# Attention of one encoder layer: softmax denominators on 128 partitions, a second PV result buffer, and a new order of taps, copies and the last quarter

## The chip, the cores and the metric

The kernel runs on one core of one Trainium2 chip. The metric is the device time of one execution in microseconds (us), as the median of three runs. A difference of about 0.3% (5.8 us) is what can be told from no change. The engines are named as the profile names them: PE (matmul), PEld (its weight loads), DVE (vector), ACT (scalar activations), POOL (GpSimd), SP (which only issues transfers here).

## The reference, cut to what matters

One encoder layer on 1024 tokens of width 1024. Between two feed-forward blocks stands a mixer whose input projection feeds two groups: a depthwise convolution of 31 taps on 512 channels, and an attention of eight heads. The change touches the attention and what is interleaved with it.

```python
def one_block(qblk):
    s = jnp.einsum('bqhd,bkhd->bhqk', qblk, k, preferred_element_type=jnp.float32) * scale
    p = jax.nn.softmax(s, axis=-1).astype(v.dtype)
    return jnp.einsum('bhqk,bkhd->bqhd', p, v)
...
a = u[..., :C_CONV] * jax.nn.sigmoid(u[..., C_CONV:])
a = lax.conv_general_dilated(a, conv_w[i], ...) + conv_b[i]     # 31 taps, depthwise
a = jax.nn.silu(_layernorm(a, g_conv_ln[i], b_conv_ln[i]))
...
mix = jnp.concatenate([a, att], axis=-1) @ w_out[i]
```

## The kernel before, in words

All engines run programs written out by hand, each in its own order; semaphores tie them together. The attention is cut into four **turns** (`i`, two heads each) of four **quarters** (`m`, one head and one half of the 512 queries each; `m` even is the first half of a head, `m` odd the second), and each quarter into four **parts** (`p`). `run_units` writes turn 0 and turn 3 out and loops over turns 1 and 2, calling each engine's own `unit`.

What PE does in a part: in even quarters it first transposes a quarter of the next head's q and k (L1710, four matmuls, into PSUM bank 7); then the scores of the next quarter once in low precision for the row maxima (`pe_max`, L1594, two matmuls); the scores proper (`pe_scores`, L1635, six matmuls); and two of the eight key tiles of PV (`pe_pv`, L1657, four matmuls into bank 6) for the quarter before. In part 3 the PV is split in two, and between the halves PE transposes the four columns of maxima into a row (`pe_max_row`, L1616).

What serves it: DVE reduces the maxima (`dve_max`, L1602) and takes the rounding rests of the transposed head (`dve_head_unit`, L1728) after ACT has copied it (`act_head_unit`, L1721). ACT copies the row of maxima (`act_max`, L1623), then takes the exponentials (`act_exp`, L1644). The values matrix carries 64 columns of ones, so that rows 0 to 63 of bank 6 are the PV result and rows 64 to 127 are 64 equal copies of the denominators, for 512 queries.

The end of a quarter's PV, in `m`'s part 3 and the next quarter: `act_pv_copy` (L1666) copies bank 6 to SBUF (`grow`) in one 128x512 instruction; `dve_pv_recip` (L1673) inverts rows 64 to 127 in three pieces of 192, 160 and 160 columns, written to rows 0 to 63; `dve_pv_scale` (L1681) multiplies 64x512 into `att`. There is one buffer, so the copy waits for the scale of the quarter before (`pv_out`), and PE's next PV waits for the copy (`pv_copied`) and for the exponentials (`s_exp`).

Interleaved is the convolution. In turns 0 to 2 ACT multiplies (`act_prod`, L1806, 10 products of 128x1024 in each head; part 3 has one, part 0 of an even quarter two) into a ring of two, and POOL adds each in two halves of 128x512 (L1815, L1816). `act_prod` waits until POOL has added the product before last. DVE does four further taps in each odd quarter (`dve_tap`, L1826, 128x1024). POOL also prepares the next head's q and k (L1760, L1762, L1766) in odd quarters. In turn 3 there are no taps and products; POOL sums and scales for the layer norm of the convolution (L1850) and scales `w_out` rows as they arrive (L1910), ACT and DVE cut them in high and low parts (L1920, L1924), DVE scales the convolution by the norm (`dve_ln_scale`, L1895), and ACT applies the swish (L1901). After the last quarter PE does the PV of the last one and goes on to the output projection (L2759), whose left operand DVE cuts from `cv` and `att` (`cut_mix`, L2565 and L2568).

## Time and profile before

| quantity | us |
|---|---|
| median of three runs | 1916.84 |
| lowest, highest run | 1915.08, 1920.34 |
| the profiled execution, its own time | 1917.73 |
| span of its profile | 1915.9 |
| mean granted TensorE clock | 0.986 of full |

A timeline row reads: start, duration of the group, engine and line, operation, what is written and read, how many, and in brackets how long the engine sat idle before it and who ended that. Consecutive instructions of one line are merged; an instruction's record starts about 0.1 us before its predecessor's record ends. PE records overlap further, so that the pitch (start to start) tells more than the duration.

### The profile page before, as it was taken

Reading aid. Unit: us, or ns where it says so; the run is one execution under the profiler, and the core shown is the slowest. Engines: PE = TensorE matmul, PEld = TensorE weight load, DVE = VectorE, ACT = ScalarE, POOL = GpSimd, SP = SyncE. Lnnn points to the kernel's source line nnn. Section 1 sums busy time; section 2 is a strip of 40 time slices with the busy share of each in tenths; the row PEclk is TensorE's granted clock in tenths of the full one; section 3 lists DMA queues with packets and bytes.
Section 4 is the critical chain, followed back from the end, with each engine's and each line's share of the span. In section 5 each row is a group of like instructions: output and inputs, shape, how many; then the busy total and the mean of one; then the engine's idle time right before and its main releaser. Section 6 shows DMA issues by size and latency. Waiting matters only on the chain.

```text
span 1915.9 us, 22675 instructions
## 1 busy us (share of the span) xinstructions
PE 1839.0 (96%) x8039; PEld 1469.6 (77%) x8039; DVE 1386.3 (72%) x1774; ACT 797.3 (42%) x1252; POOL 803.2 (42%) x605
## 2 busy tenths in 40 slices
PE   4999999999999999997999999999999999999997
PEld 3788888888888878985655666877888888888886
DVE  6678888886777785776888886358656555577778
ACT  4532232223344554237676653154332333334443
POOL 1076655665200010019999952014566556520000
PEclk9999999999999999997999999999999999999999
DMA  9046666545753442000000024112233323476333
GB/s 352 16 139 198 210 219 203 193 155 199 254 205 94 122 173 65 8 1 0 1 1 0 0 66 154 66 56 93 100 111 109 110 83 110 171 253 225 98 106 126
DMA packets 132795, 232.11 MB, mean 121 GB/s; under 512 B 8780, under 2 KB 66227, under 8 KB 132434
## 3 DMA queue, kind: packets, MB, share of 16 engines
q1 hardware_dynamic: 132500, 230.73, 35.7%
q8 instruction: 62, 1.02, 0.2%
q14 instruction: 43, 0.35, 0.1%
q10 hardware_dynamic: 190, 0.01, 0.0%
HBM read 177.75 MB, written 52.95 MB: 120 GB/s over the span
## 4 chain that ended last, share of the span: by engine, by line
PE 36%; POOL 7%; issue 6%; DVE 5%; ACT 1%; DMA 1%; POOLq 0%; ACTq 0%; DVEq 0%
PE ps L502 19%; PE ps L854 9%; PE ps L2759 5%; POOL cv L1816 3%; PE ps L1657 1%; POOL cv L1815 1%; PE ps L376 1%; POOL slot L1766 1%; PE ps L1635 1%; DVE T L935 1%; POOL rqk L1751 0%; DVE ring L479 0%; POOL slot L1762 0%; DVE H L2605 0%; POOL slot L1760 0%
## 5 line engine op out<-in xcount | busy, mean ns | idle before, releaser
L502 PE MATMUL ps<-T,ring 128*128 128x512 f32 x1920 | 441.8, 389 | 0.0
L502 PEld LDWEIGHTS ps<-T,ring 128*128 128x128 f32 x1920 | 360.4, 188 | 74.9 <-DVE ring L479 0.2
L502 PE MATMUL ps<-B,ring 128*128 128x512 f32 x1440 | 339.7, 392 | 4.6 <-DVE SG L561 3.7
L502 PEld LDWEIGHTS ps<-B,ring 128*128 128x128 f32 x1440 | 270.6, 189 | 64.4 <-issue 8.5
L954 POOL TENSOR_SCALAR stat<-stat 128x1 f32<-128x1 f32 x32 | 10.1, 315 | 548.2 <-ACT XS L879 258.8
L568 POOL TENSOR_TENSOR HID<-HID,SG 128x512 f32<-128x512 f32 x80 | 122.1, 1526 | 263.0 <-DVE HID L553 152.2
L854 PE MATMUL ps<-PW 128*128 128x512 f32 x924 | 217.3, 389 | 0.0
L854 PE MATMUL ps<-PT 128*128 128x512 f32 x900 | 212.0, 390 | 0.0
L854 PEld LDWEIGHTS ps<-PW 128*128 128x128 f32 x924 | 173.3, 188 | 36.0
L479 DVE TENSOR_TENSOR ring<-sums,ring 128x512 fp32r<-128x512 f32 x160 | 162.3, 1023 | 52.9 <-ACT ring L473 52.9
L854 PEld LDWEIGHTS ps<-PT 128*128 128x128 f32 x900 | 168.5, 188 | 34.7
L473 ACT ACTIVATE ring<-sums 128x512 fp32r<-128x512 f32 x160 | 97.1, 627 | 162.4 <-PE ps L502 144.5
L522 ACT ACTIVATE SG<-SG 128x512 f32<-128x512 f32 x80 | 50.6, 633 | 242.5 <-DVE SG L553 96.4
L1657 PE MATMUL ps<-E,vs 128*128 128x512 f32 x256 | 125.6, 606 | 5.6 <-ACT grow L1666 5.6
L479 DVE TENSOR_TENSOR ring<-rawu,ring 128x512 fp32r<-128x512 f32 x60 | 66.9, 1125 | 51.6 <-ACT ring L473 51.6
L1635 PE MATMUL ps<-qkT 97*128 97x512 f32 x384 | 102.3, 403 | 0.0
L701 ACT ACTIVATE PW<-adat 128x512 fp32r<-128x512 f32 x77 | 48.6, 631 | 123.4 <-PE ps L854 87.4
L1602 DVE TENSOR_REDUCE negmax<-ps 128x1 f32<-128x1024 f32 x64 | 76.8, 1203 | 30.5 <-PE ps L1594 30.4
L701 ACT ACTIVATE PT<-adat 128x512 fp32r<-128x512 f32 x75 | 47.4, 631 | 107.7 <-PE ps L854 92.1
L708 DVE TENSOR_TENSOR PT<-adat,PT 128x512 fp32r<-128x512 f32 x84 | 58.7, 708 | 43.2 <-ACT PT L701 43.2
L1816 POOL TENSOR_TENSOR cv<-cv,prod 128x512 f32<-128x512 f32 x60 | 89.6, 1494 | 0.0
L1635 PEld LDWEIGHTS ps<-qkT 97*128 97x128 f32 x384 | 73.8, 193 | 19.1 <-ACT qkT L1623 1.2
(337 smaller groups left out, 3307.6 us busy)
## 6 DMA issues: line engine op xcount, KB each, us to landing
adat<-ffn_hidden SPq DMA_DIRECT2D x154, 256.0 KB, 2.7
ada_raw<-in_w_ada SPq DMA_DIRECT2D x56, 512.0 KB, 4.0
rawg<-in_ffn_wg SPq DMA_DIRECT2D x22, 1024.0 KB, 5.5
rawu<-in_ffn_wu SPq DMA_DIRECT2D x22, 1024.0 KB, 5.2
ffn_hidden<-HID SPq DMA_DIRECT2D x84, 256.0 KB, 2.7
ffn_hidden<-base SPq DMA_DIRECT2D x66, 256.0 KB, 2.9
H<-in_x SPq DMA_DIRECT2D x16, 512.0 KB, 6.2
h_saved_rows<-H SPq DMA_DIRECT2D x16, 512.0 KB, 2.6
```

The source lines that it names most:

```text
L473: e.activation(ring[:, n % RING, HI], src, ACT.Copy).then_inc(f.w_hi.sem, 1)
L479: e.tensor_tensor(ring[:, n % RING, LO], src, ring[:, n % RING, HI].bitcast(F32), ALU.subtract).then_inc(f.w_lo.sem, 1)
L502: mm = e.matmul(ps[:, product_bank(M, k)], ring[:, place % RING, wx, kc], RIGHT[k][:, xx, kc], start=(kc == 0 and i == 0), stop=(kc == HC ...
L568: e.tensor_tensor(HID[:, q], HID[:, q], SG[:, q], ALU.mult).then_inc(f.w_mul.sem, 1)
L701: e.activation(pair(f, n)[:, 0, HI], left_raw(n), ACT.Copy).then_inc(f.cut_hi.sem, 1)
L708: e.tensor_tensor(pair(f, n)[:, side, LO], raw, pair(f, n)[:, side, HI].bitcast(F32), ALU.subtract)\
L854: mm = e.matmul(bank_of(j, t), pair(f, n)[:, 0, ax, t * P:(t + 1) * P], pair(f, n)[:, 1, wx], start=(g == 0 and i == 0), stop=(g == GROUPS ...
L1602: e.tensor_reduce(negmax[:, m % 2, p:p + 1], ps[:, b:b + NH].rearrange("p b k -> p (b k)"), AX_X, ALU.max, negate=True).then_inc(s_max, 1)
L1635: mm = e.matmul(ps[:, 2 + 2 * (p % 2) + b], qkT[0:AUG, hp, 1, x, kt * P:(kt + 1) * P], qkT[0:AUG, hp, 0, y, h * HALF:(h + 1) * HALF], star ...
L1657: mm = e.matmul(ps[:, 6], vs[:, hp, kt], EX[(m - 1) % 2][:, kt], start=(kt == 0), stop=(kt == NT - 1))
L1816: e.tensor_tensor(cv[:, c, second_half], cv[:, c, second_half], prod[:, n % 2, second_half], ALU.add)\
L2759: mm = e.matmul(ps[:, 4 + m % MB], mixT[:, t % 2, xx, c], wo[:, c, wx, h * HALF:(h + 1) * HALF], start=(c == 0 and k == 0), stop=(c == KC ...
```

## The change

Six things, all in the attention:

- the copy of the PV result becomes four instructions of 64x256: result and denominators of 256 queries go to rows 0 to 63 and those of the other 256 queries to rows 64 to 127, of two separate arrays in `grow`;
- each array has two buffers (`m % 2`), so the copy waits for the scale of two quarters before;
- the reciprocal is in place on 128 partitions, two pieces of 128 columns instead of three of 192, 160 and 160 on 64;
- the scale is two instructions of 64x256, done in part 2 instead of part 3;
- ACT does the copy ahead of the part's exponential instead of after it (not in the last quarter of the last turn); the DVE tap of an odd quarter's part 3 moves to the same place as those of the other parts;
- in the last turn the reciprocals and the scale of quarter 3 are all in part 0, around the two small layer norm steps, and the four layer norm scalings all in part 2.

```diff
         def act_pv_copy(e, i, m):

             e.wait_ge(pv_mm, i * 4 + m)
-            if not (isinstance(i, int) and i == 0 and m == 1):
-                e.wait_ge(pv_out, i * 4 + (m - 1))
-            e.activation(grow[:, 0:HALF], ps[:, 6], ACT.Copy).then_inc(pv_copied, 1)
+            if not (isinstance(i, int) and i == 0 and m <= 2):
+                e.wait_ge(pv_out, i * 4 + (m - 2))
+            for c in range(2):
+                of_ps = slice(c * QUERIES, (c + 1) * QUERIES)
+                for to, rows in ((pv_res, slice(0, VH)), (pv_sum, slice(VH, 2 * VH))):
+                    copied = e.activation(to[c * VH:(c + 1) * VH, m % 2], ps[rows, 6, of_ps], ACT.Copy)
+            copied.then_inc(pv_copied, 1)
...
-            a, b = ((0, 192), (192, 352), (352, HALF))[third]
-            e.reciprocal(grow[0:VH, HALF + a:HALF + b], grow[VH:2 * VH, a:b]).then_inc(pv_rec, 1)
+            x = pv_sum[:, m % 2, part * P:(part + 1) * P]
+            e.reciprocal(x, x).then_inc(pv_rec, 1)
...
-            e.tensor_tensor(dst, grow[0:VH, 0:HALF], grow[0:VH, HALF:D], ALU.mult).then_inc(pv_out, 1)
+            for c in range(2):
+                at_q = h * HALF + c * QUERIES
+                dst = att[hp * VH:(hp + 1) * VH, bass.ds(chunk, 1), at_q:at_q + QUERIES].rearrange("p a q -> p (a q)")
+                half = slice(c * VH, (c + 1) * VH)
+                scaled_rows = e.tensor_tensor(dst, pv_res[half, m % 2], pv_sum[half, m % 2], ALU.mult)
+            scaled_rows.then_inc(pv_out, 1)
...
+                    if p == 3 and not (first and m == 0) and not (last and m == 3):
+                        act_pv_copy(e, i, m)
                     act_exp(e, i, m, p)
-                    if p == 3 and not (first and m == 0):
+                    if last and (m, p) == (3, 3):
                         act_pv_copy(e, i, m)
...
-                    elif not last and p < 3:
+                    elif not last:
                         dve_tap(e, i * DTT + (DT + m // NH * 2 + p // 2), (p % 2,))
...
+                        elif not at_end and p < 2:
                             dve_pv_recip(e, *at(i, m - 1), p)
...
+                        elif not at_end and p == 2:
+                            dve_pv_scale(e, *at(i, m - 1))
```

How the rows move on DVE in an odd quarter, turn 0, quarter 3 (`negmax` the maxima of the next quarter, `cv<-ac,cw,cv` a tap, `grow` the denominators, `att` the scaled result). Before:

```order
L1602 TENSOR_REDUCE negmax<-ps 128x1
L1826 SCALAR_TENSOR_TENSOR cv<-ac,cw,cv 128x1024
L1673 RECIPROCAL grow<-grow 64x192
L1602 TENSOR_REDUCE negmax<-ps 128x1
L1826 SCALAR_TENSOR_TENSOR cv<-ac,cw,cv 128x1024
L1673 RECIPROCAL grow<-grow 64x160
L1602 TENSOR_REDUCE negmax<-ps 128x1
L1826 SCALAR_TENSOR_TENSOR cv<-ac,cw,cv 128x1024
L1673 RECIPROCAL grow<-grow 64x160
L1602 TENSOR_REDUCE negmax<-ps 128x1
L1681 TENSOR_TENSOR att<-grow 64x512
L1826 SCALAR_TENSOR_TENSOR cv<-ac,cw,cv 128x1024
```

The same quarter after:

```order
L1602 TENSOR_REDUCE negmax<-ps 128x1
L1838 SCALAR_TENSOR_TENSOR cv<-ac,cw,cv 128x1024
L1681 RECIPROCAL grow<-grow 128x128
L1602 TENSOR_REDUCE negmax<-ps 128x1
L1838 SCALAR_TENSOR_TENSOR cv<-ac,cw,cv 128x1024
L1681 RECIPROCAL grow<-grow 128x128
L1602 TENSOR_REDUCE negmax<-ps 128x1
L1838 SCALAR_TENSOR_TENSOR cv<-ac,cw,cv 128x1024
L1692 TENSOR_TENSOR att<-grow 64x256 x2
L1602 TENSOR_REDUCE negmax<-ps 128x1
L1838 SCALAR_TENSOR_TENSOR cv<-ac,cw,cv 128x1024
```

One reciprocal less stands ahead of the last maxima of the quarter, and the scale now stands behind the third tap instead of ahead of the fourth.

On ACT at the seam of two quarters, turn 0, part 3 of quarter 2 into quarter 3 (`qkT` the row of maxima, then `E` the exponentials, `prod` a product for POOL). Before:

```order
L1623 ACTIVATE qkT<-ps 1x512
L1644 ACTIVATE E<-ps 128x1024
L1666 ACTIVATE grow<-ps 128x512
L1806 ACTIVATE prod<-ac,cw 128x1024
L1644 ACTIVATE E<-ps 128x1024
```

After:

```order
L1623 ACTIVATE qkT<-ps 1x512
L1673 ACTIVATE grow<-ps 64x256 x4
L1644 ACTIVATE E<-ps 128x1024
L1818 ACTIVATE prod<-ac,cw 128x1024
L1644 ACTIVATE E<-ps 128x1024
```

The copy, four instructions now, stands between the row of maxima and the part's exponential; the product stays behind both.

On DVE in quarter 3 of the last turn and what follows it (`stat` the layer norm's variance, `wo` the low part of a `w_out` row block, `cv<-cv,ps` the layer norm scaling). Before:

```order
L1881 TENSOR_REDUCE stat<-ps 128x8
L1883 TENSOR_SCALAR stat<-stat 128x8
L1673 RECIPROCAL grow<-grow 64x192
L1924 TENSOR_TENSOR wo<-wor,wo 128x1024
L1673 RECIPROCAL grow<-grow 64x160
L1924 TENSOR_TENSOR wo<-wor,wo 128x1024
L1673 RECIPROCAL grow<-grow 64x160
L1895 TENSOR_TENSOR cv<-cv,ps 128x1024 x2
L1924 TENSOR_TENSOR wo<-wor,wo 128x1024
L1681 TENSOR_TENSOR att<-grow 64x512
L1895 TENSOR_TENSOR cv<-cv,ps 128x1024 x2
```

After:

```order
L1681 RECIPROCAL grow<-grow 128x128
L1893 TENSOR_REDUCE stat<-ps 128x8
L1895 TENSOR_SCALAR stat<-stat 128x8
L1681 RECIPROCAL grow<-grow 128x128
L1692 TENSOR_TENSOR att<-grow 64x256 x2
L1936 TENSOR_TENSOR wo<-wor,wo 128x1024 x2
L1907 TENSOR_TENSOR cv<-cv,ps 128x1024 x4
L1936 TENSOR_TENSOR wo<-wor,wo 128x1024
```

The scale of quarter 3 moves from the last but one place to ahead of the first of three `wo` cuts.

## Rows read from the trace of the kernel before

**Rows 1.** The page, part 1: busy time, share of the span, instructions.

```profile
PE 1839.0 (96%) x8039; PEld 1469.6 (77%) x8039; DVE 1386.3 (72%) x1774; ACT 797.3 (42%) x1252; POOL 803.2 (42%) x605
```

**Rows 2.** Windows (us, busy of each engine, PEclk, DMA): one head of turn 2.

```profile
1056.00:1089.00 33.00, 31.36 (x118) 19.59 (x117) 28.73 (x25) 23.19 (x28) 31.79 (x23) 1.00 0.00 0
```

**Rows 3.** Timeline of PE, turn 2, second head.

```profile
1064.43 0.64 PE L1710 MATMUL ps<-ident,slot 128*96 128x128 f32 x4 [0.93 <-DVE qkT L1728]
...
1071.84 0.65 PE L1616 MATMUL ps<-ident,negmax 128*128 128x128 f32 x4
1072.33 1.02 PE L1657 MATMUL ps<-E,vs 128*128 128x512 f32 x2
...
1075.04 1.88 PE L1657 MATMUL ps<-E,vs 128*128 128x512 f32 x4
...
1087.41 0.65 PE L1616 MATMUL ps<-ident,negmax 128*128 128x128 f32 x4 [0.65 <-DVE negmax L1602]
```

**Rows 4.** Timeline of ACT, same stretch.

```profile
1061.87 1.15 ACT L1806 ACTIVATE prod<-ac,cw 128x1024 f32 x1 [1.34 <-POOL cv L1816]
...
1073.14 1.03 ACT L1644 ACTIVATE E<-ps 128x1024 f32<-128x1024 f32 x1
1074.06 0.59 ACT L1666 ACTIVATE grow<-ps 128x512 f32<-128x512 f32 x1
1074.54 1.16 ACT L1806 ACTIVATE prod<-ac,cw 128x1024 f32 x1
```

**Rows 5.** Timeline of POOL, same stretch.

```profile
1067.84 1.28 POOL L1816 TENSOR_TENSOR cv<-cv,prod 128x512 f32<-128x512 f32 x1
...
1075.77 1.65 POOL L1815 TENSOR_TENSOR cv<-cv,prod 128x512 f32<-128x512 f32 x1 [1.21 <-ACT prod L1806]
...
1087.36 3.00 POOL L1816 TENSOR_TENSOR cv<-cv,prod 128x512 f32<-128x512 f32 x1
```

**Rows 6.** Timeline of DVE, same stretch.

```profile
1071.04 0.75 DVE L1728 SCALAR_TENSOR_TENSOR qkT<-ps,gains,qkT 96x512 fp32r<-96x512 f32 x1 [0.23 <-ACT qkT L1721]
...
1075.00 1.28 DVE L1826 SCALAR_TENSOR_TENSOR cv<-ac,cw,cv 128x1024 f32<-128x1024 f32 x1
...
1087.32 0.68 DVE L1681 TENSOR_TENSOR att<-grow 64x512 f32 x1
```

**Rows 7.** Groups with shapes apart: count, busy us, mean ns, idle before.

```profile
L1666 ACT ACTIVATE grow<-ps 128x512 f32<-128x512 f32 x16 | 9.5, 592 | 6.8 <-DVE att L1681 5.1 <-PE ps L1657 1.7
...
L2212 ACT ACTIVATE tmp<-ps 128x256 f32<-128x256 f32 x8 | 3.1, 391 | 0.0
...
L1673 DVE RECIPROCAL grow<-grow 64x160 f32<-64x160 f32 x32 | 36.3, 1140 | 0.8
...
L2463 DVE TENSOR_TENSOR rt<-kr 128x256 f32<-128x256 f32 x1 | 0.4, 419 | 0.0
```

**Rows 8.** Timeline of all engines, last turn, quarter 2 to the projection.

```profile
1124.74 1.95 PE L1657 MATMUL ps<-E,vs 128*128 128x512 f32 x4 [0.54 <-ACT grow L1666]
...
1134.07 3.33 POOL L1850 TENSOR_TENSOR pp<-pp 128x1024 f32<-128x1024 f32 x1
...
1137.48 2.38 POOL L1850 TENSOR_TENSOR pp<-prod,pp 128x1024 f32<-128x1024 f32 x1
...
1153.09 1.01 ACT L1644 ACTIVATE E<-ps 128x1024 f32<-128x1024 f32 x1
...
1154.47 2.84 DVE L1681 TENSOR_TENSOR att<-grow 64x512 f32<-64x512 f32 x1
...
1158.14 9.57 PE L1657 MATMUL ps<-E,vs 128*128 128x512 f32 x16 [4.78 <-ACT grow L1666]
```

**Rows 9.** Windows again, and one PE row: where the clock is low.

```profile
1160.00:1163.00 3.00, 3.00 (x5) 1.32 (x4) 2.97 (x3) 3.00 (x5) 0.69 (x1) 0.50 0.97 415
...
711.65 0.50 PE L376 MATMUL ps<-xh,W 128*128 128x512 f32 x1 [2.01 <-DVE xl L996]
...
713.50:716.00 2.50, 2.50 (x7) 1.92 (x7) 0.00 (x0) 2.50 (x3) 1.18 (x20) 0.51 0.00 0
```

More of the change, by code:

```diff
@@ L1659, in pe_pv, with dve_pv_recip @@
                 mm.then_inc(pv_mm, 1)
+        QUERIES = HALF // 2
+        pv_res = grow[:, 0:HALF].rearrange("p (b q) -> p b q", b=2)
+        pv_sum = grow[:, HALF:D].rearrange("p (b q) -> p b q", b=2)
         def act_pv_copy(e, i, m):
             e.wait_ge(pv_mm, i * 4 + m)
-            if not (isinstance(i, int) and i == 0 and m == 1):
-                e.wait_ge(pv_out, i * 4 + (m - 1))
-            e.activation(grow[:, 0:HALF], ps[:, 6], ACT.Copy).then_inc(pv_copied, 1)
-        def dve_pv_recip(e, i, m, third):
-            if third == 0:
+            if not (isinstance(i, int) and i == 0 and m <= 2):
[5 more added lines that the diff above has]
+            copied.then_inc(pv_copied, 1)
+        def dve_pv_recip(e, i, m, part):
+            if part == 0:
                 e.wait_ge(pv_copied, i * 4 + m)
-            a, b = ((0, 192), (192, 352), (352, HALF))[third]
-            e.reciprocal(grow[0:VH, HALF + a:HALF + b], grow[VH:2 * VH, a:b]).then_inc(pv_rec, 1)
+            x = pv_sum[:, m % 2, part * P:(part + 1) * P]
+            e.reciprocal(x, x).then_inc(pv_rec, 1)
         def dve_pv_scale(e, i, m):
@@ L1678, in dve_pv_scale @@
             chunk = i if m >= 1 else i - 1
-            e.wait_ge(pv_rec, i * 12 + 3 * m)
-            dst = att[hp * VH:(hp + 1) * VH, bass.ds(chunk, 1), h * HALF:(h + 1) * HALF].rearrange("p a q -> p (a q)")
-            e.tensor_tensor(dst, grow[0:VH, 0:HALF], grow[0:VH, HALF:D], ALU.mult).then_inc(pv_out, 1)
+            e.wait_ge(pv_rec, i * 8 + 2 * m)
+            for c in range(2):
[4 more added lines that the diff above has]
+            scaled_rows.then_inc(pv_out, 1)
         def act_v(e, i, hp, first=False):
@@ L2569, in cut_mix @@
                                 ALU.subtract).then_inc(mix_lo, 1)
-            for third in range(3):
-                dve_pv_recip(e, TURNS, -1, third)
+            for part in range(2):
+                dve_pv_recip(e, TURNS, -1, part)
             dve_pv_scale(e, TURNS, -1)
@@ L2576, in _ @@
             dve_wo_lo(e, KC - 2)
-            for third in range(3):
-                dve_pv_recip(e, TURNS, 0, third)
+            for part in range(2):
+                dve_pv_recip(e, TURNS, 0, part)
             dve_pv_scale(e, TURNS, 0)
```

25 lines of the change are left out of this document (8 added, 17 removed).

## The prediction

> **What bounds the kernel now.** I read four views, in this order. The page's busy line says that PE is the engine to save time on: 96% of the span [rows 1]. A change that only shortens DVE instructions is therefore worth what PE waits for DVE, and no more. The windows of one head in the steady turns show PE busy 31.36 of 33.00 us, but POOL 31.79 of 33.00 [rows 2]: PE has 1.6 us of slack per head, POOL 1.2 us. The timelines then show which engine closes the loop. The reader is to follow one head from 1061.87. ACT's product there has waited for POOL's add, 1.34 us; behind it in ACT's queue stands the copy of the transposed head, behind that DVE's rest, and PE's next transposes start at 1064.43 after 0.93 us of waiting for that rest [rows 3, 4]. PE then runs on to the row of maxima at 1071.84, ACT takes the exponential at 1073.14, the PV copy at 1074.06 and only then the product at 1074.54 [rows 3, 4], and POOL, which has sat idle 1.21 us for it, starts at 1075.77 [rows 5]. Its next idle time is one head later. So the loop is: POOL's string of adds, ACT's product, head copy, PE, row of maxima, ACT's queue at the **even seam** (end of an even quarter), POOL. Whatever is added to ACT there is added to the head. At the **odd seam** PE waits 0.65 us for DVE's last maxima [rows 3]; that wait is off the loop, since POOL is busy all through it (its add at 1087.36 takes 3.00) [rows 5].
>
> The last turn has no products. There the view is the timeline around the last quarter: PE ends the PV of quarter 2's result at about 1153.4, and starts the last PV at 1158.14 after 4.78 us idle, released by the copy, which waited for DVE's scale (1154.47, 2.84 us) [rows 8]. That is the largest single stall that the change can remove.
>
> **The change part by part.**
>
> *Reciprocals.* Three pieces of 192, 160 and 160 columns become two of 128. A piece of 160 takes 1.14 us [rows 7]; in proportion 128 columns are 0.91, and with a small fixed part I take 0.93 us. DVE loses some 3.6 and gains 1.9 us per quarter. It frees DVE ahead of the last maxima of an odd quarter (one piece of 1.14 less, shorter others, a scale of some 0.8 more: 1.0 us in all), which covers the 0.65 us wait at the odd seam. By the loop above I price this at nothing: what is late next is POOL. Bounds: 0 to -0.65 x 6 seams = -3.9 us.
>
> *The copy on ACT.* One 128x512 copy takes 592 ns, and the next instruction starts 0.48 behind it [rows 4, 7]. A 256-column instruction takes 391 ns, an accumulating one of 128 partitions [rows 7]; with the same overlap of 0.11 it costs 0.27-0.28 us, four cost 1.1 us against 0.48. The PE ends the PV at 1072.33 + 1.02 = 1073.35 [rows 3], so the copies, now ahead of the exponential, run 1073.4 to 1074.5, the exponential (0.92 from start to start) to 1075.4, and the product starts at 1075.4 in place of 1074.54: **+0.87 us** for POOL. Against that, POOL's first add at 1075.77 took 1.65 where the undisturbed one takes 1.28 [rows 5], because DVE's tap of 1075.00 to 1076.28 [rows 6] was still running; by then it will be over: -0.38. Net +0.5 us per even seam. PE's PV at 1075.04 [rows 3] will wait for the exponential until about 1075.5, another 0.5 us, in an odd quarter where it had 0.65 to spare.
>
> The Trainium skill ("VectorE: DVE Perf Modes", section on the TRN2 errata) gives 172 cycles plus one per column at 1.2 GHz for ScalarE from PSUM: an estimate of 0.36 us for 256 columns, and 0.57 for 512 where the trace has 0.592. By it the seam would cost some 0.1 us less.
>
> *The scale, moved from part 3 to part 2.* In an even quarter it now stands where POOL's add of 1067.84 is due, which took its undisturbed 1.28 [rows 5]. DVE instructions with two SBUF inputs and POOL's adds lengthen each other in this trace: POOL's add at 1087.36 took 3.00, 1.72 more, beside a scale of 0.68 and a tap [rows 5, 6]. Two scales of 256 columns take 0.42 each [rows 7], 0.77 together, so POOL loses about 0.7 ahead of the add that the second product of part 2 waits for. Behind that product stand the head copy and DVE's rest (1071.04 + 0.75 = 1071.79 [rows 6]), and the row of maxima at 1071.84 [rows 3] had only 0.2 us of slack against PE's own work. That is **+0.5 us** more per even seam. Bounds 0 (POOL's loss hidden) to +0.7. In odd quarters scale and tap only change places, 0.
>
> The five even seams with a PV copy in turns 0 to 2 thus give 5 x (0.5 + 0.5) = **+5.0 us**, with ends -0.2 x 5 and +1.6 x 5.
>
> *Double buffering in the steady turns.* All 16 copies together waited 5.1 us for the scale [rows 7], and nearly all of that is in the last turn. Worth nothing before it.
>
> *Last turn, quarters 0 to 2.* No POOL slack hides ACT here. At each seam the exponential that the next PV needs comes later: about +0.45 into quarter 0 (through the head copy), +0.5 into quarter 1, +0.55 into quarter 2, where PE waited for the copy already (1124.74) [rows 8]. In quarter 2, the scale now comes ahead of DVE's cut of `w_out`, which has two SBUF inputs as well. POOL's layer norm sum at 1134.07 took 3.33, the next one 2.38 [rows 8]; I put the 0.95 between them down to that cut, the scale adds its 0.8, and PE waits for these sums: +0.9 with what the maxima lose. Quarter 3's PV is released a little earlier, -0.2. Sum of 0.45, 0.5, 0.55, 0.9 and -0.2: **+2.2 us**, ends 0 and +3.5.
>
> *The end.* The copy of quarter 3 waits for a scale long done. The exponential at 1153.09 still stands ahead of it, to 1154.0 [rows 8], then four copies to 1155.2, and the PV starts at about 1155.25 in place of 1158.14: **-2.9 us**. What is late next is the projection's first operand: exponential, copies, table load, four swishes and two cuts end some 7 us behind 1154, at about 1161; the PV needs until 1162 at least, so this is covered by one us. The 16 PV matmuls at 1158.14 ran with the granted clock at 0.50, the lower of the two levels, 1.2 GHz [rows 9]; from 1158.14 to 1167.15 they took 9.0 us where groups of four elsewhere have a pitch of 1.72, or 6.9. Would the shorter idle time of 1.9 us keep the clock high, another -2.1 us came with it. But an idle time of 2.01 us was followed by a clock of 0.51 too [rows 9]. That row is the nearest, so I take 0 and keep -2.1 for the range.
>
> **Sum.** 5.0 + 2.2 - 2.9 = +4.3 us. The profiled execution took 1917.73, 0.9 above the median; on it the sum gives 1922.0, on the median of 1916.84 it gives **1921.1**.
>
> **The rivals.**
> *A, PE's waits for DVE were the bound* (faster). If the odd seam's 0.65 counts, and ACT's extra work hides in POOL's adds, the steady turns give -0.65 x 6 = -3.9 in place of +5.0; with the end's -2.9, a kept clock -2.1 and +2.2 it is -6.7: 1910.1. For it: DVE is busy 28.73 of 33.00 [rows 2] and PE names it twice [rows 3]. Against: POOL's own gap is 1.21 us in a head.
> *B, steady turns even, clock kept*: 0 + 2.2 - 5.0 = -2.8: 1914.0.
> *C, POOL gets in between the two scales* (slower). Then a scale pair lasts 0.4 + 1.3 + 0.4 = 2.1 in place of 0.8, 1.3 more, in odd quarters ahead of the last maxima; the 1.0 us that DVE gained is used up, and the odd seam's wait grows by 0.3 to 1.3 us. Over six heads, with about 0.7 of it reaching the loop, +4 on top of the forecast: 1925. It decides as soon as more than 1.0 us is lost between the two. Against it: in the trace a scale and the tap behind it kept POOL out together (0.68 + 1.27 against 1.72 lost) [rows 5, 6].
> The Trainium skill ("SBUF — State Buffer", section "Who interferes with whom") says that whichever of the two starts first holds the shared port for its whole instruction, which speaks for a slip at each boundary, two now where there was one; by that rule the time is C's.
> *D, the stall at the end only changes its name* (the swishes or the cuts hold the projection): the -2.9 is lost, 1924.0.
>
> **How the numbers follow.** The forecast with its own range of 1918 to 1925 has 0.47, A 0.18, B 0.13, C 0.14, D 0.08. The bounds are 1911.1 and 1922.6 (0.3% of 1916.84, about what can be told from no change). Of the forecast's 0.47 a third lies beyond 1922.6, as do C and most of D: slower 0.33. Of A a little over three quarters lies below 1911.1, with a little of B: faster 0.15. The rest, 0.52, is within 0.3%. The range to hold 8 in 10 leaves out half of A and part of C: 1911 to 1925.5.
>
> **What would show it.** The profile after should show: four 64x256 copies of 0.36-0.39 us; POOL idle about 2 us for `prod` once a head instead of 1.21, and the head's period up from about 33.5 to 34.5; PE waiting for `E` (exponentials), not for `grow`, at seams; PE no longer waiting for `negmax` at odd seams; an idle time of about 1.9 us instead of 4.78 ahead of the last PV. It is wrong if the period of a head stays or falls (then A or B), or if single 64x256 scales last over 1 us in odd quarters (C).

## The result, and the profile after

The changed kernel takes **1946.01 us** in the median (1941.86 to 1947.98) against 1916.84: the ratio is 1.0145 with a 95% interval of 1.0131 to 1.0159. By that ratio it is slower by 28 us, where the forecast was +4.3, and outside the range of 1911.0 to 1925.5. The profiled execution took 1941.86 (span 1940.0), 24.1 more than that of before.

To find the place I cut both traces at the same events: the starts of the sixteen rows of maxima on PE (L1616; "turns 0 to 2" below are from the third to the thirteenth), the start of the last PV, the start of the output projection. A number in this table is the difference of two starts in the timeline, in us.

| stretch | before | after | difference |
|---|---|---|---|
| start to the first row of maxima | 885.7 | 886.6 | +0.9 |
| first to third | 35.6 | 33.1 | -2.5 |
| turns 0 to 2 (third to thirteenth) | 166.1 | 186.5 | **+20.4** |
| last turn to its last PV | 70.7 | 75.8 | **+5.1** |
| last PV to projection | 9.0 | 9.2 | +0.2 |
| projection to end | 748.8 | 748.8 | +0.1 |

All the kernels below but b_best and b_best2 have the same order in the first two lines, and yet the first line runs from 884.0 to 888.2 us and the second from 33.1 to 35.7. In the trace of before, PE stops 2.50 us at the second row of maxima and the six matmuls of scores behind it take 2.93 us; in that of after it stops 0.91 and they take 1.65. So these differences are no effect of the change. The loss is in the steady turns, and some of it in the last one.

The page, part 1, and the windows of one whole head, from one transpose of it (PE L1722) to the same of the next. The columns are those of [rows 1] and [rows 2].

```profile
PE 1840.1 (95%) x8039; PEld 1468.0 (76%) x8039; DVE 1387.2 (72%) x1774; ACT 812.4 (42%) x1300; POOL 797.8 (41%) x605
```

```profile
1070.40:1107.63 37.23, 32.39 (x122) 19.93 (x121) 29.57 (x25) 25.58 (x33) 31.56 (x24) 1.00 0.00 0
```

A head takes 37.2 us where it took 33.5. No engine's busy time grew by anything like that: against the 33.00 us of [rows 2], which are half a us short of a whole head, PE has 1.0 us more, DVE 0.8, POOL none. PE is now idle 4.8 us in a head and POOL 5.7. So the head got longer by waits. Who waits for whom, from the list of waits of the whole trace (waiting engine and line, the one that ended the wait, total us, times, longest):

```profile
PE ps L1616 <- DVE negmax L1602: 15.2, 7, 3.5
PE ps L1657 <- ACT E L1644: 10.1, 14, 1.5
PE ps L1616 <- DVE qkT L1740: 6.4, 6, 1.2
```

```profile
POOL cv L1827 <- ACT prod L1818: 29.8, 12, 3.9
```

In the trace of before the first was 4.3, the second was not in the list, the third 2.5, and POOL's 10.0. The waits of 15.2 and 6.4 us have grown most on PE, apart from that for the exponentials, and both stand at the row of maxima. The timeline there, all engines that take part, one even seam and one odd seam (the stretch is that of the window above):

```profile
1081.79 1.27 POOL L1827 TENSOR_TENSOR cv<-cv,prod 128x512 f32<-128x512 f32 x1
...
1082.59 3.43 DVE L1692 TENSOR_TENSOR att<-grow 64x256 f32 x2
1083.02 1.27 POOL L1828 TENSOR_TENSOR cv<-cv,prod 128x512 f32<-128x512 f32 x1
1084.30 1.43 POOL L1827 TENSOR_TENSOR cv<-cv,prod 128x512 f32<-128x512 f32 x1
1085.70 1.45 POOL L1828 TENSOR_TENSOR cv<-cv,prod 128x512 f32<-128x512 f32 x1
1085.94 1.21 DVE L1602 TENSOR_REDUCE negmax<-ps 128x1 f32<-128x1024 f32 x1
1087.18 0.75 DVE L1740 SCALAR_TENSOR_TENSOR qkT<-ps,gains,qkT 96x512 fp32r<-96x512 f32 x1
1087.98 0.65 PE L1616 MATMUL ps<-ident,negmax 128*128 128x128 f32 x4 [0.99 <-DVE qkT L1740]
...
1089.53 1.55 ACT L1673 ACTIVATE grow<-ps 64x256 f32<-64x256 f32 x4 [0.28 <-PE ps L1657]
...
1092.37 1.96 PE L1657 MATMUL ps<-E,vs 128*128 128x512 f32 x4 [1.01 <-ACT E L1644]
...
1093.24 1.27 POOL L1827 TENSOR_TENSOR cv<-cv,prod 128x512 f32<-128x512 f32 x1 [3.65 <-ACT prod L1818]
...
1102.03 2.92 DVE L1692 TENSOR_TENSOR att<-grow 64x256 f32 x2
...
1104.87 1.21 DVE L1602 TENSOR_REDUCE negmax<-ps 128x1 f32<-128x1024 f32 x1
...
1106.21 0.65 PE L1616 MATMUL ps<-ident,negmax 128*128 128x128 f32 x4 [2.05 <-DVE negmax L1602]
```

How to read it. The pair of scales is 0.77 us of work and lasts 3.43. Its two records end at 1084.58 and 1086.02, each just inside a POOL add that began 0.3 us earlier and that is 0.16 to 0.18 longer than its undisturbed 1.27. So POOL pays 0.35 us for the pair and DVE 2.7. Read from these rows, each of the two waits until an add of POOL ends; the first, begun at 1082.59, even missed the boundary at 1083.02. Behind the pair stand the last row maxima and the last head rest, and the row of maxima on PE waits for these (0.99 us, at the odd seam 2.05). The products for POOL stand behind that row in ACT's queue, so POOL idles 3.65 us for the next one, where it idled 1.21 [rows 5]. The granted clock plays no part in it here: it is 1.00 over the whole of turns 0 to 2.

### The profile page after: what moved, and what is told of

Read it like the earlier page. It is cut to its first block, busy times and chain, and to the rows that moved or that the text cites. A ratio compares the mean times of both kernels' runs of the same rounds, so it can differ in the third digit from the quotient of the medians.

```text
span 1940.0 us, 22728 instructions
## 1 busy us (share of the span) xinstructions
PE 1840.1 (95%) x8039; PEld 1468.0 (76%) x8039; DVE 1387.2 (72%) x1774; ACT 812.4 (42%) x1300; POOL 797.8 (41%) x605
## 4 chain that ended last, share of the span: by engine, by line
PE 39%; DVE 9%; issue 3%; ACT 2%; POOL 1%; DMA 0%; DVEq 0%; ACTq 0%; POOLq 0%
PE ps L502 18%; PE ps L854 9%; PE ps L2767 4%; PE ps L1657 3%; DVE att L1692 1%; PE ps L1635 1%; DVE cv L1838 1%; PE ps L376 1%; DVE negmax L1602 1%; ACT grow L1673 1%; ACT E L1644 1%; DVE qkT L1740 1%; PE ps L1594 1%; DVE T L935 0%; PE ps L1616 0%
## 5 line engine op out<-in xcount | busy, mean ns | idle before, releaser
L1657 PE MATMUL ps<-E,vs 128*128 128x512 f32 x256 | 126.2, 609 | 13.9 <-ACT E L1644 10.1
L1827 POOL TENSOR_TENSOR cv<-cv,prod 128x512 f32<-128x512 f32 x60 | 78.1, 1302 | 30.2 <-ACT prod L1818 29.8
L1828 POOL TENSOR_TENSOR cv<-cv,prod 128x512 f32<-128x512 f32 x60 | 90.3, 1505 | 0.0
```

The source lines that it names most:

```text
L1657: mm = e.matmul(ps[:, 6], vs[:, hp, kt], EX[(m - 1) % 2][:, kt], start=(kt == 0), stop=(kt == NT - 1))
L1827: e.tensor_tensor(cv[:, c, first_half], cv[:, c, first_half], prod[:, n % 2, first_half], ALU.add)
L1828: e.tensor_tensor(cv[:, c, second_half], cv[:, c, second_half], prod[:, n % 2, second_half], ALU.add)\
```

## The experiments

Every kernel was compared with the kernel before on the same chip. The table gives ratio and interval, and from the profile of each the stretches defined above. Three kernels whose steady turns are alike (the kernel before, and the double buffer with either order of the end) give 166.1, 166.2 and 166.0. But a kernel that reaches the third row of maxima early, as the changed one does, may give some of that back in turn 0; so where a reading rests on less than 2 us, I go by the eight rows from the fifth to the thirteenth, four whole heads, which take 134.0 us before and 149.4 after. From the projection to the end all take 748.5 to 748.8 us, save b_dbuf_early with 751.6 and b_best2 with 756.7.

| kernel | ratio | turns 0-2 | last turn | last PV to projection |
|---|---|---|---|---|
| before | 1 | 166.1 | 70.7 | 9.0 |
| after | 1.0145 [1.0131, 1.0159] | 186.5 | 75.8 | 9.2 |
| a_p3 | 1.0022 [1.0007, 1.0036] | 170.9 | 73.4 | 8.2 |
| a_one | 1.0034 [1.0020, 1.0048] | 174.0 | 71.6 | 7.5 |
| a_late | 1.0137 [1.0120, 1.0154] | 185.0 | 77.3 | 9.2 |
| b_split | 1.0036 [1.0020, 1.0052] | 168.7 | 74.4 | 9.4 |
| b_place | 1.0021 [1.0012, 1.0030] | 171.7 | 70.3 | 8.1 |
| b_place_split | 1.0115 [1.0100, 1.0130] | 184.0 | 75.4 | 8.0 |
| b_copy4 | 1.0039 [1.0025, 1.0054] | 170.8 | 75.6 | 9.4 |
| b_dbuf | 0.9988 [0.9977, 0.9999] | 166.2 | 66.9 | 10.2 |
| b_dbuf_early | 0.9996 [0.9985, 1.0006] | 167.7 | 66.4 | 10.2 |
| b_dbuf_end | 1.0008 [0.9995, 1.0021] | 166.0 | 69.5 | 8.3 |
| b_best | 1.0002 [0.9989, 1.0016] | 163.1 | 70.1 | 8.2 |
| b_best2 | 0.9990 [0.9977, 1.0002] | 170.1 | 66.2 | 6.5 |

A name with a_ is the changed kernel with one edit, one with b_ the kernel before with one or a few.

### Is it the split of the scale or its place?

**a_p3**: the changed kernel with the scales back in part 3 (in odd quarters ahead of the tap).

```diff
-                    elif not last:
+                    elif not last and p < 3:
                         dve_tap(e, ...)
...
-                        elif not at_end and p == 2:
+                        elif not at_end and p == 3:
                             dve_pv_scale(e, *at(i, m - 1))
+                    if m % NH == 1 and p == 3 and not last:
+                        dve_tap(e, ...)
```

> The changed kernel, with the two scales back in part 3 (ahead of the tap in odd quarters), as the kernel before has its one. If the loss is the pair's length wherever it stands (theory 1 as it was put): within 3 us of the changed kernel's 1946. If it is length times place (in part 2 the last row maxima and, in even quarters, the last head rest stand right behind the pair; in part 3 only work that is not yet due does): 10 to 18 us under it, some 1928 to 1934, PE's waits for the row maxima back to some 4 us in all.

Measured: 1921.13 us. Of the 28 us, 24 are back by the ratios, more than the 10 to 18 expected. DVE's timeline through one head:

```profile
1077.81 2.85 DVE L1692 TENSOR_TENSOR att<-grow 64x256 f32 x2
1080.59 1.21 DVE L1602 TENSOR_REDUCE negmax<-ps 128x1 f32<-128x1024 f32 x1
...
1093.12 1.83 DVE L1692 TENSOR_TENSOR att<-grow 64x256 f32 x2
1094.98 2.18 DVE L1838 SCALAR_TENSOR_TENSOR cv<-ac,cw,cv 128x1024 f32<-128x1024 f32 x1
```

The pair still lasts 2.85 and 1.83 us. It is not cured, it is out of the way: what stands behind it is the first row maxima of the next quarter, which are not due for some time, or a tap, for which nobody waits. PE's wait for the last maxima falls from 15.2 us to 1.3:

```profile
PE ps L1616 <- DVE negmax L1602: 1.3, 1, 1.3
```

**a_one**: the changed kernel with one 128x256 scale in place of the pair. It puts the result of the second 256 queries into rows 64 to 127 of `att`, which is not their place; the rest is computed as before.

```diff
-            for c in range(2):
-                ...
-                scaled_rows = e.tensor_tensor(dst, pv_res[half, m % 2], pv_sum[half, m % 2], ALU.mult)
+            e.tensor_tensor(dst, pv_res[:, m % 2], pv_sum[:, m % 2], ALU.mult).then_inc(pv_out, 1)
```

> The changed kernel, with the two scales of 64x256 replaced by one of 128x256 (which puts the second 256 queries in the wrong rows of the attention output: the output is not the layer's, the time of everything else is). Theory 1: one wait for a POOL add in place of two, 1.0 to 1.4 us less on DVE per quarter: 8 to 14 us under the changed kernel's 1946. Rivals 2 and 3: within 2 us of it.

Measured: 1922.56 us, turns 0 to 2 at 174.0. One instruction at the same place costs 12.5 us less there than two, and by the ratios 21 us less in all, where 8 to 14 were expected. The groups of turns 1 and 2 (count, busy us, mean ns, idle before), first after, then a_one:

```profile
L1692 DVE TENSOR_TENSOR att<-grow 64x256 f32 x16 | 25.1, 1569 | 0.2
```

```profile
L1690 DVE TENSOR_TENSOR att<-grow 128x256 f32 x8 | 14.2, 1781 | 0.0
```

A mean of 1569 ns for 0.42 us of work, and 1781 ns for the single piece: it waits about as long for POOL as each of the two halves does. Splitting doubles the number of waits, not the work.

**b_split**, **b_place**, **b_place_split**: the same from the other side. b_split makes the scale of the kernel before two instructions of 64x256 at its old place, b_place moves it whole to part 2 in turns 0 to 2, b_place_split does both.

```diff
-            e.tensor_tensor(dst, grow[0:VH, 0:HALF], grow[0:VH, HALF:D], ALU.mult).then_inc(pv_out, 1)
+            e.tensor_tensor(dst[:, 0:mid], grow[0:VH, 0:mid], grow[0:VH, HALF:HALF + mid], ALU.mult)
+            e.tensor_tensor(dst[:, mid:HALF], grow[0:VH, mid:HALF], grow[0:VH, HALF + mid:D], ALU.mult).then_inc(pv_out, 1)
```

```diff
-                        if p == 3:
+                        if p == 3 and last:
                             dve_pv_scale(e, *at(i, m - 1))
-                        elif not (last and m == 2 and p == 2):
+                        elif p < 3 and not (last and m == 2 and p == 2):
                             dve_pv_recip(e, *at(i, m - 1), p)
+                        if p == 2 and not last:
+                            dve_pv_scale(e, *at(i, m - 1))
```

> The kernel before, with the scale of 64x512 as two of 64x256 at the same place; nothing else. Theory 1 (each half-row scale waits for one of POOL's adds, some 1.4 us): a pair lasts 2.3 to 3.4 us here too and the median rises by 6 to 12 us. Rival 2 (the copies on ACT cost the 28 us): within 2 us of before. Rival 3 (it is the place in part 2 that costs, not the split): a pair lasts under 1.6 us, as the single one does (mean 1.2), within 2 us.

> The kernel before with one edit: in turns 0 to 2 the scale (still one 64x512 instruction) follows the third reciprocal in part 2 instead of standing in part 3. Copy, buffer and reciprocals are as before. Theory (what costs is the length of the scale times its place; the place alone is worth little while the scale is one instruction): one scale of 0.7 to 2.9 us behind POOL's add ahead of the last row maxima; turns 0 to 2 take 167 to 170 us (166.1 before), the median 1.0005 to 1.002 of before. Rival 1 (the place alone carries the loss, whatever the number of pieces): turns 0 to 2 take 176 or more, the ratio 1.005 or more. Rival 2 (place is harmless when the reciprocals stand in thirds, the 0.65 us wait at the odd seam is unchanged): 166 us, 1.000.

> The kernel before with the scale in part 2 in turns 0 to 2, as in b_place, and made of two instructions of 64x256 everywhere. Theory (length times place): in part 2 the pair lasts 2.9 to 3.4 us as in the changed kernel, and DVE still has a third reciprocal there, so the last maxima come later: turns 0 to 2 take 176 to 184 us, the median 1.006 to 1.011 of before, far more than the +2.6 us of the split in part 3 and the cost of the place alone together. Rival (the two edits add up, and the loss of the changed kernel needs the four copies on ACT as well): 169 to 172 us, 1.003 to 1.005.

Measured over the 166.1 us of before: the split alone +2.6, the place alone +5.6, both **+17.8**. Were they to add up it would be 8.2. The place alone cost more than I had expected of it (up to 4), but its ratio of 1.0021 is far from the 1.005 of the rival that wanted all of the loss there. The odd seam of b_place and that of b_place_split:

```profile
1088.38 1.60 DVE L1681 TENSOR_TENSOR att<-grow 64x512 f32 x1
...
1091.24 0.65 PE L1616 MATMUL ps<-ident,negmax 128*128 128x128 f32 x4 [2.44 <-DVE negmax L1602]
```

```profile
1102.47 1.32 DVE L1682 TENSOR_TENSOR att<-grow 64x256 f32 x1
1103.72 1.47 DVE L1683 TENSOR_TENSOR att<-grow 64x256 f32 x1
...
1106.46 1.11 PE L1616 MATMUL ps<-ident,negmax 128*128 128x128 f32 x4 [3.56 <-DVE negmax L1602]
```

Even seams differ more: in b_place the one scale lasts its undisturbed 0.68 us there (at 1071.04) and PE has no wait at the row of maxima; in b_place_split the pair lasts 1.9 us and PE waits 0.83, and POOL's idle time for products goes from 12.7 to 28.8 us in all. From there the delay passes through ACT's product to POOL.

A part of the 17.8 is another thing, the clock. Behind the odd seam's stop of 3.6 us it fell to the lower level, 1.2 GHz, at three of the four odd seams inside turns 0 to 2. One of them (PEclk is the number behind POOL's):

```profile
1068.90:1072.00 3.10, 3.01 (x8) 1.80 (x9) 2.20 (x2) 1.76 (x3) 1.12 (x1) 0.50 0.00 0
```

The rows behind these stops came 19.0 to 19.3 us later, the row behind the one odd seam that kept its clock (a stop of 2.42) 17.7 us later. That is some 1.4 us each time, about 4 us in all. b_place lost its clock once, at 953.37, for about the same 1.4. Without these, split and place cost 2.6 and about 4.2 apart, and 13 to 14 together, still twice the sum. The changed kernel has 1.00 there, so of its 20.4 us the split and the place account for those 13 to 14, and the copies (next experiment) for most of the rest; this is an estimate from the rows. b_place_split also keeps the third reciprocal ahead of its scale, which the changed kernel has not.

In b_split the pair stands at its old place, behind the last maxima, and lasts 2.1 us in the mean. The last turn is 3.7 us longer: ACT's copy, which has one buffer there, waits for the second half of the scale, PE stops 2.45 us for the copy ahead of quarter 3's first PV (0.24 before), and the clock behind that stop is 0.57 for 4 us.

### The four copies on ACT

**b_copy4**: the kernel before with the four 64x256 copies at their old place behind the exponential. **a_late**: the changed kernel with its copies there too.

```diff
-            e.activation(grow[:, 0:HALF], ps[:, 6], ACT.Copy).then_inc(pv_copied, 1)
+            for c in range(2):
+                cols = slice(c * (HALF // 2), (c + 1) * (HALF // 2))
+                for rows in (slice(0, VH), slice(VH, 2 * VH)):
+                    copied = e.activation(grow[rows, cols], ps[rows, 6, cols], ACT.Copy)
+            copied.then_inc(pv_copied, 1)
```

```diff
-                    if p == 3 and not (first and m == 0) and not (last and m == 3):
-                        act_pv_copy(e, i, m)
                     act_exp(e, i, m, p)
-                    if last and (m, p) == (3, 3):
+                    if p == 3 and not (first and m == 0):
                         act_pv_copy(e, i, m)
```

> The kernel before, with the PV copy as four instructions of 64x256, behind the exponential as it was; nothing else. Rival 2 (ACT at the seams): four take 1.55 us in place of 0.59, the product for POOL and the next head copy come 1 us later at every seam, the median rises by 4 to 10 us. Theory 1 alone: within 2 us of before.

> The changed kernel, with the copies behind the exponential again, as before. Rival 2: PE's PV no longer waits for the exponential behind four copies (0.4 to 1.2 us at each of 14 seams in the changed kernel), but it waits for the copies themselves; 2 to 8 us under 1946. Theory 1 alone: within 2 us of it.

Measured: b_copy4 +4.7 us in turns 0 to 2, a_late -1.5 against the changed kernel there and +1.5 in the last turn; its ratio of 1.0137 is not to be told from 1.0145, where 2 to 8 us were expected. The group of the copies in b_copy4:

```profile
L1669 ACT ACTIVATE grow<-ps 64x256 f32<-64x256 f32 x64 | 24.1, 376 | 6.3 <-DVE att L1685 3.7 <-PE ps L1657 2.1
```

64 copies in 24.1 us, four in 1.5 as in the changed kernel (1.55 at 1089.53): they do not overlap, where one 128x512 copy costs the queue 0.48. That is +1.1 us for each quarter of ACT's queue. A product or an exponential is late behind them either way: POOL's wait for products goes from 10.0 to 16.6 us in b_copy4, and PE waits for the copy in both kernels (11.2 and 9.1 us in all, 5.6 before) where it waits 10.1 us for the exponential in the changed one. Whether the place of the copies matters can't be read from a_late alone: its odd seams have stops of 2.2 to 2.3 us, behind which the clock often fell (0.72 in the window 1102 to 1108, and 0.95 over turns 0 to 2), where the changed kernel's stops of 2.0 to 2.1 left it at 1.00. b_dbuf_early below, without such falls, says that the place costs nothing while the copy is one instruction.

### The end

**b_dbuf**: the kernel before with the second buffer alone, made from a free array: one 128x512 copy, DVE's order as before. **b_dbuf_early**: that, with the copy ahead of the exponential. **b_dbuf_end**: b_dbuf with DVE's order in the last quarter like that of the change (reciprocals and scale in part 0, four norm scalings in part 2).

```diff
-            if not (isinstance(i, int) and i == 0 and m == 1):
-                e.wait_ge(pv_out, i * 4 + (m - 1))
-            e.activation(grow[:, 0:HALF], ps[:, 6], ACT.Copy).then_inc(pv_copied, 1)
+            if not (isinstance(i, int) and i == 0 and m <= 2):
+                e.wait_ge(pv_out, i * 4 + (m - 2))
+            e.activation(tmp[:, m % 2], ps[:, 6], ACT.Copy).then_inc(pv_copied, 1)
```

> The kernel before with the second PV result buffer alone (the copy goes to a free array of two buffers, one 128x512 instruction, and waits for the scale of two quarters before); the order on every engine is that of before. Theory: turns 0 to 2 unchanged at 166; idle ahead of the last PV 1.8 instead of 4.8 us with the clock high in it, and the gain handed to a wait for the first cut of the projection's operand (about 3 us), since the norm scalings, three reciprocals and a scale stand ahead of it on DVE: 0.9995 to 1.0005. Rival (the stall's removal reaches the end): 0.9975, 1912.

> The kernel before with two buffers for the PV result and the copy (one of 128x512) ahead of the part's exponential, as the change has it; DVE's order as before. If the new order on ACT costs by itself: PE's PV waits for the exponential 0.3 to 0.5 us at each seam, the product for POOL comes 0.3 later, head period 33.8 to 34.2, the median 2 to 5 us over before. If not: within 2 us, or under it by what the single buffer cost at the end.

> The kernel before with two things of the change alone: two buffers for the PV result (one copy of 128x512, three reciprocals on 64 partitions and one scale as before, in other memory), and the last quarter's order on DVE. If the end's gain is real and was hidden by the rest: the idle time ahead of the last PV falls from 4.8 to 1 to 2 us, the clock stays high through it as in the run with one scale, the median is 3 to 6 us under before; head period 33.5 as before. If a w_out row block holds the exponential there (as in the changed kernel, ACT 3.97 us for POOL): within 2 us of before.

The end of b_dbuf, from the timeline, and the clock while its last PV runs (PEclk in the window):

```profile
1152.09 1.06 ACT L1920 ACTIVATE wo<-wor 128x1024 fp32r<-128x1024 f32 x1 [2.62 <-POOL wor L1910]
1153.05 1.00 ACT L1644 ACTIVATE E<-ps 128x1024 f32<-128x1024 f32 x1
...
1154.69 7.11 PE L1657 MATMUL ps<-E,vs 128*128 128x512 f32 x16 [1.82 <-ACT tmp L1666]
1157.21 2.33 DVE L1895 TENSOR_TENSOR cv<-cv,ps 128x1024 f32<-128x1024 f32 x2
...
1159.57 3.37 DVE L1673 RECIPROCAL grow<-tmp 64x192 f32<-64x192 f32 x3
...
1164.90 3.48 PE L2759 MATMUL ps<-wo,mixT 128*128 128x512 f32 x14 [3.11 <-DVE mixT L2568]
```

```profile
1158.00:1161.00 3.00, 3.00 (x8) 1.33 (x7) 2.97 (x4) 2.24 (x3) 2.35 (x1) 1.00 0.96 404
```

The second buffer does what the prediction said: 1.82 us idle in place of 4.78 [rows 8]. The clock stays at its upper level, 2.4 GHz, and the sixteen matmuls take 7.1 us in place of 9.6. Both together bring the last PV's end forward by some 6 us. But DVE still has two norm scalings, three reciprocals and a scale ahead of the first cut of the projection's operand, and PE waits 3.11 us for that cut. What is left is the ratio of 0.9988, 2.3 us, with an interval that ends at 0.9999; expected was 0.9995 to 1.0005.

b_dbuf_early took 1916.77 us, a ratio of 0.9996. Its four whole heads take 133.9 us as in b_dbuf (134.1), so the copy ahead of the exponential costs a steady head nothing. The +1.6 in its turns 0 to 2 is all in turn 0, behind a first stretch 1.7 us shorter. The end has the same stops of 1.78 and 3.11 us, but here the second was followed by the lower level, where b_dbuf kept 1.00, and the projection takes 3.1 us longer:

```profile
1165.00:1168.00 3.00, 2.33 (x6) 1.85 (x7) 2.94 (x5) 1.35 (x2) 0.00 (x0) 0.51 0.85 366
```

b_dbuf_end (1917.38 us, ratio 1.0008, as its rival had it) takes the norm scalings away from there, and meets another stall:

```profile
1155.22 1.06 ACT L1920 ACTIVATE wo<-wor 128x1024 fp32r<-128x1024 f32 x1 [5.48 <-POOL wor L1910]
1156.19 1.01 ACT L1644 ACTIVATE E<-ps 128x1024 f32<-128x1024 f32 x1
...
1157.82 8.56 PE L1657 MATMUL ps<-E,vs 128*128 128x512 f32 x16 [4.32 <-ACT tmp L1666]
```

The last exponential stands behind ACT's cut of a `w_out` block. That waits for POOL's scaling of the block, POOL for its transfer (5.10 us), and the transfer for the buffer that DVE frees with its own cut. In b_dbuf_end that cut is late, because the scale of quarter 3 now stands ahead of it. The changed kernel has the same chain:

```profile
1176.05 4.67 POOL L1922 TENSOR_TENSOR wor<-wor,gm_row 128x1024 f32<-128x1024 f32 x2 [4.74 <-DMA wor<-in_w_out]
...
1178.45 1.06 ACT L1932 ACTIVATE wo<-wor 128x1024 fp32r<-128x1024 f32 x1 [3.97 <-POOL wor L1922]
1179.42 1.00 ACT L1644 ACTIVATE E<-ps 128x1024 f32<-128x1024 f32 x1
...
1180.32 1.53 ACT L1673 ACTIVATE grow<-ps 64x256 f32<-64x256 f32 x4
...
1182.00 8.44 PE L1657 MATMUL ps<-E,vs 128*128 128x512 f32 x13 [3.76 <-ACT grow L1673]
```

3.76 us idle, not 1.9, and a clock of 0.50 behind it (1182 to 1185). That the transfer waits for DVE's cut is in the list of waits of b_dbuf_end (`SPq L2023 <- DVE wo L1924`); no kernel was run with a further buffer for `w_out`.

### A version that beats both?

**b_best**: b_dbuf_end, and in turns 0 to 2 the last product of an even quarter ahead of ACT's row of maxima, so that POOL has no gap there. **b_best2**: b_dbuf with the same, and on DVE at the end the last norm scalings ahead of the scale, and the projection's first two cuts ahead of the reciprocals of the last but one result.

```diff
+                    if p == 3 and m % NH == 0 and not last:
+                        for n in products(m, p, p + 1):
+                            act_prod(e, i, n, first)
                     if p == 3 and not (last and m == NU - 1):
                         act_max(e, i, m + 1)
```

> As the run with two buffers and the last quarter's order, and in even quarters ACT's last product goes ahead of the row of maxima, where ACT is idle 1.5 us, so that POOL does not wait 1.2 us for it. If POOL's string of adds with the gap in it is the loop of the kernel before: POOL's idle time for the product falls under 0.5 us in a head, head period 32.3 to 32.9, some 4 to 6 us under the run without it. If it is not: the same median within 2 us.

> b_dbuf with two more edits. First: in turns 0 to 2 the product of part 3 of even quarters goes ahead of ACT's row of maxima. Second: on DVE at the end the last two norm scalings go ahead of the scale of quarter 2's result, and the projection's first two cuts go ahead of the three reciprocals and the scale of quarter 3's. Theory: turns 0 to 2 take 163 us as in b_best, row of maxima to last PV 17.5 us, last PV to projection 7 to 7.5 us (no wait for the cut), projection to end 749 to 750: 1909 to 1912, a ratio of 0.996 to 0.9975. Rival (the end's stall moves on once more, to DVE's cut for the attention half of the operand, or to a w_out block): last PV to projection 7.5 and projection to end 751 to 752, so 0.9985.

Measured: 1915.67 and 1916.56 us, neither to be told from before, so both missed the gain that was expected. In b_best a head is shorter by 0.7 us and turns 0 to 2 by 3.0. Its window of [rows 2]:

```profile
1056.00:1089.00 33.00, 32.14 (x122) 20.00 (x121) 27.47 (x25) 23.88 (x28) 33.00 (x24) 1.00 0.00 0
```

POOL is busy all of the time, and that has its price. The timeline of b_best2 in turn 0:

```profile
936.33 1.30 POOL L1815 TENSOR_TENSOR cv<-cv,prod 128x512 f32<-128x512 f32 x1
936.36 8.58 DVE L1681 TENSOR_TENSOR att<-tmp,grow 64x512 f32<-64x512 f32 x1
...
942.89 1.51 POOL L1766 TENSOR_TENSOR slot<-qn,rqk 128x768 f32<-128x768 f32 x1
944.87 1.21 DVE L1602 TENSOR_REDUCE negmax<-ps 128x1 f32<-128x1024 f32 x1
...
946.13 1.22 PE L1594 MATMUL ps<-qkT 96*128 96x512 f32 x2 [4.31 <-DVE negmax L1602]
```

One scale of 0.68 us lasts 8.58, through seven POOL instructions without a gap, until POOL runs dry; PE waits 4.31 us, the clock behind that is 0.50 (946 to 950), and turn 0 loses some 7. The profiled execution is one of the longest of twelve, which spread from 1910.27 to 1921.69; that such an event decides which of them is short fits, but only one of them was traced. A tap of 5.73 us stands in the traces of both b_best and b_best2 at about 906, beside POOL instructions that follow each other as closely. At the end of b_best2 the cut is no longer waited for (6.5 us from last PV to projection), and PE stops 5.08 us for the operand's attention half instead, whose reciprocals had been put back; with the lower clock behind that stop (0.50 in 1175 to 1180) the projection to the end takes 7.9 us more. b_dbuf is the one version whose interval lies below 1, by 0.1%, which is less than the 0.3% of the first section.

## Why the prediction was wrong

**Right.** *Reciprocals*: 0.93 us was taken for 128x128, the group shows 0.939. That the time so freed on DVE is worth nothing by itself was not tried alone. *The loop through POOL, ACT's product and the row of maxima* [rows 2 to 5]: b_best takes POOL's gap away and the head falls from 33.5 to 32.8 us. *The end's stall*: the second buffer removes it, as b_dbuf shows (below). That a_p3, with the scales out of the way, has +4.8 us in turns 0 to 2, near the +5.0 of the sum, is luck: half of the 5.0 was for the moved scale, which a_p3 does not have, and the copies, priced at 2.5, make +4.7 alone in b_copy4.

**The step that failed** is "The scale, moved from part 3 to part 2", in three places.

- The duration. "Two scales of 256 columns take 0.42 each, 0.77 together, so POOL loses about 0.7": POOL loses 0.35, and DVE 2.1 to 2.7 us, for a pair in the steady heads. I had read who yields from one row, the scale of 0.68 beside a POOL add of 3.00 [rows 5, 6]. The group of the scales of turns 1 and 2 in the same trace said otherwise, and I did not use it (the kernel before, columns as in [rows 7]):

```profile
L1681 DVE TENSOR_TENSOR att<-grow 64x512 f32 x8 | 9.2, 1156 | 0.2
```

  A mean of 1156 ns beside a 0.68 in the timeline means that a scale often waits: the four at even seams last 1.57 to 1.70 us, the four at odd seams 0.68 or 0.69. DVE or POOL may be the one that yields, and the mean over all of them was the number to use.
- "In odd quarters scale and tap only change places, 0." The tap of part 3 is behind the last maxima, and the scale is now ahead of them. b_place has +5.6 us for that and its like in even quarters (1.4 of it the clock), and PE's wait at the odd seam goes from 0.65 us to 2.44.
- The interaction that was missing: the cost of length and place together is more than their sum. The pair behind the maxima costs little, a single scale ahead of them lasts its undisturbed 0.68 us at even seams, and only the pair ahead of them delays PE at both seams. 2.6 and 5.6 apart are 17.8 together, or 2.6, 4.2 and 13 to 14 without the falls of the clock.

**Rival C** named the mechanism and the point, "as soon as more than 1.0 us is lost between the two", and mis-sized it. It had the pair at 2.1 us in odd quarters alone, with "about 0.7 of it reaching the loop": +4 on top of the forecast. The pair is 2.92 there and 3.43 in even quarters, so both halves wait and not only the second, and a head grows by 3.7 us (DVE loses 4.8 to the two pairs; slack covers a part, and the copies add theirs). The evidence against C was the same single pair of rows. The rule of the Trainium skill behind it ("SBUF — State Buffer", section "Who interferes with whom"), an exclusive lock on the shared port, agrees with the durations: each half is held until an add ends (1.99 and 1.43 us for the two records of the pair at 1082.59). The trace adds what happens at a boundary: at 1083.02 POOL's next add got in ahead of the scale that had waited since 1082.59.

**ACT's term** was mis-sized as well: four copies were put at 1.1 us, with the overlap of a 128x512 copy, and are 1.55. PE waits for exponentials, as forecast, 1.01 us at the even seam in place of the 0.5 forecast.

**The last turn**: quarters 0 to 2 were put at +2.2; the thirteenth to the sixteenth row of maxima take 6.7 us more. 4.7 of these are in quarter 2, where the pair again stands ahead of the last maxima: it lasts 3.65 us, the `w_out` cut behind it 3.26, and PE waits 3.51; most of the rest is PE's stop of 1.54 us for the exponential (0.54 before). a_p3 and a_one have 2.7 and 2.5 in that quarter, but not for one reason: a_p3 has no wait for the maxima and loses its clock behind the same stop of 1.54 us (0.57 in 1134 to 1138), as b_copy4 does (2.6), while a_one keeps the clock and waits 1.36 us for the maxima.

**The end**: the mechanism was right, and b_dbuf shows it with the size forecast (1.82 us idle) and with the kept clock that the prediction had as a bound of its range. In the changed kernel the -2.9 became -1.7 (the sixteenth row of maxima to the last PV, 20.1 in place of 21.8 us). The prediction let the exponential start as before, and did not follow the moved scale to the `w_out` cut behind it, whose buffer a transfer needs. That is the kind of thing rival D had, with another culprit: ACT's `w_out` cut and the transfer before it, rather than swishes and cuts of the operand. DVE's queue ahead of the cuts of the operand is what stops b_dbuf.

**A and B** fall: PE's wait for the last maxima at the odd seam did not vanish with a shorter reciprocal, it trebled (0.65 to 2.05), and the steady turns did not stay even.

Of what was to show each step right or wrong: copies 0.378 us (0.36 to 0.39 forecast); POOL idle 3.65 (2); head 37.2 (34.5); PE waiting for `E` at seams (yes); no wait for `negmax` at odd seams (no, 2.05); idle ahead of the last PV 3.76 (1.9). "It is wrong if single 64x256 scales last over 1 us in odd quarters": they do.

## What to carry to other kernels

A DVE instruction with two SBUF inputs beside a busy POOL can cost a wait for one of POOL's instructions, however short it is: count such instructions, not only their columns, and be slow to split one where POOL runs. Put it behind, not ahead of, what another engine waits for; taking the pair from ahead of the last maxima to behind them (a_p3) gave back 24 of 28 us, and splitting a scale that stood behind them (b_split) cost 2.6 us of the steady turns. Take the price of an instruction from its group's mean in the trace, and where one row stands far below that mean, ask who paid there. And look at the granted clock behind every stop of PE before two kernels are compared.

## What the runs showed of the hardware that was not expected

- Between DVE and POOL the one that waited was mostly DVE where a scale of the changed kernel met POOL's adds: the adds of 1.27 us grew by 0.16 to 0.18 us when a scale got in, the scales of 0.42 us took 1.4 to 2.0. The add of 3.00 in [rows 5] is the other case. Against a POOL queue without gaps a scale of 0.68 us lasted 8.58 and a tap of 1.27 lasted 5.73. So an engine without gaps is not only full: it locked its neighbour out at times. Whether the gap of 1.2 us per head that the kernel before has on POOL is of use to DVE was not tested.
- Four 64x256 copies from PSUM on ACT take 0.378 us each and do not overlap (1.55 for four). The same data in one 128x512 instruction is 0.59, and 0.48 to the next instruction.
- The length of PE's stop alone does not tell whether the clock falls. A stop of 1.82 us left it at its upper level (1.00) in b_dbuf, where 2.01 us elsewhere had been followed by 0.51 [rows 9], and 4.32 us in b_dbuf_end by 0.54 in the window 1158 to 1161. The same stop of 3.11 us was followed by 1.00 in b_dbuf and by 0.51 in b_dbuf_early, and the same one of 1.54 us by 1.00 in the changed kernel and by 0.57 in a_p3. Such a fall cost 1.4 us at a seam and 3 us at the projection.
